# A hybrid transformer block on one core: attention moved in among the qkv slabs, its bias added by VectorE, its forget sums made by a scan

## The chip, the core and the metric

The kernel runs on one NeuronCore of a Trainium2 chip. The metric is the device time of one execution in microseconds (us), lower is better; of several runs the median counts. TensorE is called PE below, VectorE DVE, ScalarE ACT, GpSimd POOL and SyncE SP.

## The reference, cut to what matters

Two layers over 256 positions of width 1024, in float32. The change touches the attention of the first:

```python
h = rmsnorm(x, ln1)
z = h @ w_in     # q, k, v of branches a, b, c, four forget columns fb, gates ga, gb, gc
o_a = moba_attention(qa, ka, va, tbl_a)                     # 4 heads of 64, causal, + bias by distance
o_b = forgetting_attention(qb, kb, vb, fb + b_f)            # 4 heads: logit[t,s] += sum_{s<j<=t} log sigmoid(f_j)
o_c = sliding_window_sink_attention(qc, kc, vc, sinks, tbl_c)  # 8 heads, 2 kv heads, window 128, bias, sink
merged = sigmoid(ga)*(o_a @ w_pa) + sigmoid(gb)*(o_b @ w_pb) + sigmoid(gc)*(o_c @ w_pc)
x = x + merged @ w_o
```

After it come a gated feed-forward part with a short convolution, and the second layer (a recurrence, cross attention, feed-forward).

## The kernel before

The weights are cut into 126 slabs of 128x2048 numbers. SP loads them into four buffers (raw), ACT rounds a slab into w_hi (L442), DVE subtracts to get w_lo (L843), and PE makes three products for each wanted one (L1438 to L1440: hi x hi, hi x lo, lo x hi). w_hi and w_lo have two buffers each, so slab n+2 can be split only when PE has used slab n (slab_used). ACT and DVE work through lists written by hand: a call of splits(m) splits all slabs up to m at that place of the engine's list, and whatever stands behind it waits. The result of a slab is a unit, held in PSUM bank 0 or 1 in turn, and ACT evacuates it.

The order around the change is: slabs 0 to 8 hold q, k and v (L1510 on), the last of them also the keys and values of branch c. Then PE makes the four forget columns with the activations stationary and four columns moving (48 products, L1521 on). DVE and ACT make the logarithm of the sigmoid from them, DVE copies it 128 columns wide (neglog_wide, L930), PE makes running sums with triangular masks (L1533 to L1535). Then follow twelve gate slabs in four batches of three. Sixteen heads go in four groups of four: group 0 is branch a, 1 is b, 2 and 3 are c. scores(g) makes the products of a group one head at a time in banks 2 and 3: queries by keys (L1549, 64 rows deep, fp32), and into the same bank the bias by a product with a mask that turns it around (L1559), or the forget sums (L1553, L1556). DVE copies each head out (L952; L946 and L948 for branch b) and finds the maxima (L957, L958); ACT takes the exponentials (L528); DVE normalises. After the next batch of gate slabs PE transposes the probabilities (prob_transposes, L1568) and multiplies by the values (weighted_values, L1580 and L1581), with ACT's copy of the transposed tile in between (pT, L540). scores(0) stands ahead of the first batch, scores(g+1) right behind the values of group g. The last group's values stand right ahead of stage proj, whose products read the attention's output and whose results DVE multiplies with the gates.

POOL makes the bias: PE and ACT make one row of it per head, POOL writes the rows to memory and reads them back shifted by one per partition (L400 to L406, bias_scratch to bias).

## Time and profile before

| | before |
|---|---|
| median of 3 runs | 1018.44 us (1017.45 to 1018.93) |
| profiled execution, its own time | 1017.91 us |
| its span, first to last instruction | 1015.7 us |
| mean granted TensorE clock | 0.958 |
| PE busy | 921.7 us, 91% |
| DVE, ACT, POOL busy | 569.8 (56%), 446.3 (44%), 17.5 (2%) |

Busy time of PE is that of its matmuls; their ends are modelled, so 91% is not a distance to a peak. A granted clock of 1.00 is 2.4 GHz, one of 0.50 is 1.2 GHz. In a row of the timeline the bracket at the end says how long the engine was idle before and what ended the wait; an fp32 product is two instructions and appears as x2. Times in a window row are of the window only.

### The profile page before, as it was taken

To read this page: it belongs to the slowest core of one execution; us is meant where nothing else is said; L and a number is where in the kernel's file an instruction comes from. 1 tells how busy PE (TensorE), PEld (TensorE's weight loads), DVE (VectorE), ACT (ScalarE), POOL (GpSimd) and SP (SyncE) were. 2 spreads that over 40 slices of the span, in tenths; PEclk is the share of its full clock that TensorE was granted. 3 is DMA by queue.
4 is the path that set the end of the run, shared out by engine and by line. 5 is a ranking of instruction groups with operands and counts; after the bars stand their busy time and mean duration, and the time that the engine had idled before them with its cause. 6 is when DMAs were issued, how large, how long until landed. Compare 5 with 4: busy or idle time off the path is not lost.

```text
span 1015.7 us, 18816 instructions
## 1 busy us (share of the span) xinstructions
PE 921.7 (91%) x8050; PEld 838.3 (83%) x8050; DVE 569.8 (56%) x693; ACT 446.3 (44%) x580; POOL 17.5 (2%) x24
## 2 busy tenths in 40 slices
PE   2998999998979999999898889987898799999996
PEld 1997877787769999988798788876796599999885
DVE  2331434456657787754759987545644545555443
ACT  4342353642455655553537330135544544343433
POOL 1100000000000000000200000000000000000000
PEclk9996899999989999999899999998999989999999
DMA  8651222332544554555453221122440435455541
GB/s 313 230 196 49 84 84 83 125 125 84 171 179 166 181 191 168 194 187 194 149 186 124 86 85 45 47 81 83 152 164 38 167 117 193 165 184 187 185 147 41
DMA packets 20925, 142.93 MB, mean 141 GB/s; under 512 B 2446, under 2 KB 2490, under 8 KB 4608
## 3 DMA queue, kind: packets, MB, share of 16 engines
q1 hardware_dynamic: 18720, 134.23, 38.3%
q0 software_dynamic: 2000, 6.74, 1.9%
q8 instruction: 51, 0.84, 0.3%
q10 hardware_dynamic: 144, 1.05, 0.3%
q14 instruction: 10, 0.08, 0.0%
HBM read 140.94 MB, written 1.07 MB: 140 GB/s over the span
## 4 chain that ended last, share of the span: by engine, by line
PE 75%; DVE 12%; ACT 8%; issue 3%; DMA 1%; SPq 0%; ACTq 0%; DVEq 0%
PE ps L1438 21%; PE ps L1440 20%; PE ps L1439 20%; DVE w_lo L843 4%; ACT w_hi L442 3%; PE ps L1756 2%; PE ps L1549 2%; PE ps L1559 2%; PE ps L1466 1%; PE ps L1706 1%; ACT sc L528 1%; DMA x<-in_x 1%; ACT xn L455 1%; PE ps L1580 1%; DVE xn L1351 1%
## 5 line engine op out<-in xcount | busy, mean ns | idle before, releaser
L843 DVE TENSOR_TENSOR w_lo<-raw,w_hi 128x2048 fp32r<-128x2048 f32 x126 | 289.6, 2299 | 195.2 <-ACT w_hi L442 195.2
L1438 PE MATMUL ps<-hT_hi,w_hi 128*128 128x256 f32 x1240 | 358.4, 289 | 7.0 <-DVE w_lo L843 7.0
L1439 PE MATMUL ps<-hT_lo,w_hi 128*128 128x256 f32 x1240 | 354.9, 286 | 0.0
L1440 PE MATMUL ps<-hT_hi,w_lo 128*128 128x256 f32 x1240 | 354.5, 286 | 0.0
L442 ACT ACTIVATE w_hi<-raw 128x2048 fp32r<-128x2048 f32 x126 | 240.6, 1910 | 153.4 <-PE ps L1440 152.7
L1438 PEld LDWEIGHTS ps<-hT_hi,w_hi 128*128 128x128 f32 x1240 | 242.5, 196 | 11.5 <-issue 10.9
L1439 PEld LDWEIGHTS ps<-hT_lo,w_hi 128*128 128x128 f32 x1240 | 242.4, 195 | 0.2
L1440 PEld LDWEIGHTS ps<-hT_hi,w_lo 128*128 128x128 f32 x1240 | 242.1, 195 | 0.0
L1438 PE MATMUL ps<-w_hi,gT_hi 128*128 128x512 f32 x176 | 69.7, 396 | 0.2 <-DVE w_lo L843 0.2
L1440 PE MATMUL ps<-w_hi,gT_lo 128*128 128x512 f32 x176 | 69.0, 392 | 0.0
L1439 PE MATMUL ps<-w_lo,gT_hi 128*128 128x512 f32 x176 | 68.4, 388 | 0.0
L1438 PE MATMUL ps<-w_hi,hT_hi 128*128 128x512 f32 (+2 forms) x144 | 52.3, 363 | 7.7 <-DVE hT_lo L897 7.7
L1466 PE MATMUL ps<-masks,xn 128*128 128x128 f32 x96 | 19.8, 377 | 42.6 <-DVE xn L880 31.2
L1061 DVE SCALAR_TENSOR_TENSOR ub<-ps,pvec,ub 128x255 f32<-128x255 f32 (+1 forms) x88 | 38.4, 478 | 29.6 <-ACT ub L584 26.7
L1466 PEld LDWEIGHTS ps<-masks,xn 128*128 128x128 f32 x96 | 15.6, 193 | 46.1 <-DVE xn L880 16.5
L1439 PE MATMUL ps<-w_lo,hT_hi 128*128 128x512 f32 (+2 forms) x144 | 52.0, 361 | 0.0
L1440 PE MATMUL ps<-w_hi,hT_lo 128*128 128x512 f32 (+2 forms) x144 | 51.8, 360 | 0.0
L584 ACT ACTIVATE ub<-ps,pvec 128x256 f32<-128x256 f32 x44 | 22.5, 561 | 54.5 <-PE ps L1440 54.5
L1440 PEld LDWEIGHTS ps<-w_hi,gT_lo 128*128 128x128 f32 x176 | 33.0, 188 | 7.7
L1438 PEld LDWEIGHTS ps<-w_hi,gT_hi 128*128 128x128 f32 x176 | 33.1, 188 | 7.4 <-DVE w_lo L843 0.9
L1439 PEld LDWEIGHTS ps<-w_lo,gT_hi 128*128 128x128 f32 x176 | 33.0, 188 | 7.2
L1438 PEld LDWEIGHTS ps<-w_hi,hT_hi 128*128 128x128 f32 x144 | 27.9, 194 | 12.4 <-issue 8.6
(289 smaller groups left out, 1145.0 us busy)
## 6 DMA issues: line engine op xcount, KB each, us to landing
raw<-in_weights SPq DMA_DIRECT2D x126, 1024.0 KB, 4.9
row_gain<-in_rows_vec POOLq DMA_DIRECT2D x4, 512.0 KB, 4.7
bias<-bias_scratch POOLq DMA_DIRECT2D x1, 1536.0 KB, 11.3
masks<-in_masks ACTq DMA_DIRECT2D x1, 1025.5 KB, 7.8
x<-in_x SPq DMA_DIRECT2D x2, 512.0 KB, 8.1
xn<-in_mem POOLq DMA_DIRECT2D x2, 512.0 KB, 4.2
out<-x SPq DMA_DIRECT2D x2, 512.0 KB, 2.6
bias<-bias_scratch POOLq DMA_DIRECT2D x1, 768.0 KB, 6.8
```

Of the source, the lines that this page charges most:

```text
L442: A(w_hi[:, n % SPLIT, :], raw[:, n % RAW, :], ACT.Copy).then_inc(sems["hi_ready"], 1)
L455: A(ub[:, 1, :, :, :].rearrange("p a b n -> p (a b n)") if name == "mem" else xn[:, t, :], src(t), ACT.Square, accum_out=stat[:, 4 * q + t ...
L584: A(ub[:, p % 2, s, c, :], src[:, c * T:(c + 1) * T], ACT.Identity, bias=pvec[:, bass.ds(p + 2 * turn, 1), col + 3], scale=pvec[:, bass.ds ...
L843: V.tensor_tensor(w_lo[:, n % SPLIT, :], raw[:, n % RAW, :], w_hi[:, n % SPLIT, :].bitcast(F32), ALU.subtract).then_inc(sems["lo_ready"], 1)
L1061: ins = V.scalar_tensor_tensor(out=dst, in0=src[:, c * T:(c + 1) * T - lag], scalar=pvec[:, bass.ds(p + 2 * turn, 1), 4 * (2 * s + c) + ta ...
L1438: mm(dst, left[0], right[0], start=first, stop=False)
L1439: mm(dst, left[0], right[1], start=False, stop=False)
L1440: return mm(dst, left[1], right[0], start=False, stop=last)
L1466: last = nc.tensor.transpose(ps[:, transposed_bank(name, k), k % 2 * T + t * P:k % 2 * T + (t + 1) * P], xn[:, t, k * P:(k + 1) * P], ident)
L1549: mm(dst[:, cols], qkT[rows, qtile, qt * P:(qt + 1) * P], qkT[rows, ktile, 0:(qt + 1) * P], start=True, stop=False)
L1559: last = mm(dst[:, cols], m("turn"), bias[:, b, cols], start=False, stop=True)
L1756: last = mm(ps[to, b + q, j * CHUNK:(j + 1) * CHUNK], left[rows, 8 * q + j, :], right(rows, 8 * q + j), start=True, stop=True)
```

## The change

- The order of the columns of w_in is changed, so that the slab with keys and values of branch c is the seventh and the queries of branch c come after it. The forget columns are no longer a unit of their own.
- forget_gates, behind slab 2: the forget columns are stationary (4 wide), the activations move (256 columns), 24 products into bank 6, on four partitions. DVE and ACT make the logarithm there, on 4x256 numbers (tile forget), and DVE makes the running sum with a scan.
- forget_sums, behind slab 4: two products turn the sums into columns and four spread them over 128 partitions in banks 6 and 7. DVE adds both and the causal mask into the score tile of group 1 ahead of its scores.
- scores(g) writes four heads into banks 2 to 5, two heads in turn: one uses rows 0 to 63, the other rows 64 to 127, so that neighbouring instructions use different halves. It makes only the products of queries and keys.
- DVE adds the bias to two heads in one instruction, reading the tile bias backwards along its columns; for group 1 it adds what stands in the score tile already.
- Attention starts behind slab 2: scores(0) there, the values of group 0 behind slab 5, of 1 behind slab 8, of 2 behind the fourth gate slab, of 3 behind the eighth. Four gate slabs follow.
- ACT's and DVE's lists are rewritten to fit. ACT's exponentials of a group are cut into two halves, each of two heads; its splits run one slab further ahead, splits(n0 + i + 2) ahead of the evacuation of unit i.
- The masks cum and turn (384 columns) are no longer loaded; the tile masks keeps the width that the later masks need. The bias rows are stored in the other direction, and POOL's two loads of bias have other widths and the same bytes.

```diff
--- before.py
+++ after.py
-              ("causal", 384), ("cum", 2 * P), ("turn", P))
+              ("causal", 384))
...
-        neglog_wide = sb("neglog_wide", [P, TT, 4, P], F32, attention)
+        forget = sb("forget", [4, 4, T], F32, attention)
...
-            for first, place, width in ((0, P, P), (P, 0, 2 * P)):
-                src = bass.AP(bias_scratch.tensor, place, [[1, P], [BIAS_ROW, 12], [1, width]])
+            for first, width in ((0, 2 * P), (2 * P, P)):
+                src = bass.AP(bias_scratch.tensor, 0, [[1, P], [BIAS_ROW, 12], [1, width]])
                 pool.dma_start(bias[:, :, first:first + width], src).then_inc(sems["bias_in"], 16)
...
+            qkv_parts = ((0, scale), (2, 1.0), ("v", 0), (4, scale), (6, 1.0), ("v", 256), ("kv", 512), (8, scale), (10, scale))
+            def qkv_out(i):
+                dst, s = qkv_parts[i]
...
+            def exps(g, heads):
                 act.wait_ge(sems["negmax_ready"], g + 1)
-                for i in range(4):
+                for i in heads:
                     for qt in range(TT):
                         s, e = (0, P) if qt == 0 else (P, 3 * P)
                         col = qt * 16 + 4 * g + i
                         A(sc[:, g % 2, i, s:e], sc[:, g % 2, i, s:e], ACT.Exp, bias=ast[:, 88 + col:89 + col],
                           accum_out=ast[:, 120 + col:121 + col]).then_inc(sems["probs_ready"], 1)
-                if g >= 2:
+                if g >= 2 and heads[-1] == 3:
...
+            for i in range(3):
+                splits(n0 + i + 1)
+                qkv_out(i)
+            splits(n0 + 4)
+            act.wait_ge(sems["z_ready"], 1)
+            A(forget[:, 1, :], forget[:, 1, :], ACT.Exp).then_inc(sems["e_ready"], 1)
+            act.wait_ge(sems["e_ready"], 1)
+            A(forget[:, 1, :], forget[:, 1, :], ACT.Ln, bias=m("ones_all")[0:4, 0:1]).then_inc(sems["log1p_ready"], 1)
+            for g in range(2):
+                exps(g, (0, 1))
+                for i in range(3 * g + 3, 3 * g + 6):
+                    splits(n0 + i + 2)
+                    qkv_out(i)
+                    if i == 3 * g + 3:
+                        exps(g, (2, 3))
+                outputs(g)
             n0, u0 = FIRST_SLAB["gates"], FIRST_UNIT["gates"]
-            splits(n0 + 1)
-            exps(0)
...
+            for i in range(12):
+                if i in (0, 4):
+                    exps(2 + i // 4, (0, 1))
+                splits(n0 + i + 2)
+                evacuated(u0 + i, A(sig[:, 2 * i:2 * i + 2, :].rearrange("p a n -> p (a n)"), unit(u0 + i),
+                                    ACT.Sigmoid))
+                if i in (1, 5):
+                    exps(2 + i // 4, (2, 3))
+                elif i in (3, 7):
+                    outputs(2 + i // 4)
...
+            n0 = FIRST_SLAB["qkv"]
+            splits(n0 + 4)
+            dve.wait_ge(sems["fb_ready"], 1)
+            do(V.tensor_scalar(forget[:, 0, :], ps[0:4, 6, 0:T], vec[0:4, VEC["b_f"]:VEC["b_f"] + 1], None, ALU.add))
             settle()
-            V.tensor_tensor(ast[:, 32:40], ast[:, 0:8], ast[:, 8:16], ALU.min).then_inc(sems["z_ready"], 1)
-            dve.wait_ge(sems["e_ready"], 1)
...
+            V.scalar_tensor_tensor(out=forget[:, 1, :], in0=forget[:, 0, :], scalar=-1.0, in1=forget[:, 0, :], op0=ALU.mult,
+                                   op1=ALU.min).then_inc(sems["z_ready"], 1)
+            do(V.tensor_scalar(forget[:, 0, :], forget[:, 0, :], 0.0, None, ALU.min))
             def maxima(g):
                 kind, _ = HEAD_GROUPS[g]
                 if g >= 2:
                     dve.wait_ge(sems["pT_ready"], 4 * (g - 1))
-                for i in range(4):
-                    h = 4 * g + i
...
+                for pair in range(2):
+                    dve.wait_ge(sems["scores_ready"], 4 * g + 2 * pair + 2)
+                    dst = sc[:, g % 2, 2 * pair:2 * pair + 2, :]
+                    b = 2 * pair + (0 if kind == "A" else 4 * (g - 1))
+                    added = dst if kind == "B" else bias[:, b:b + 2, ::-1]
+                    V.tensor_tensor(dst, ps[:, 2 + 2 * pair:4 + 2 * pair, 0:384], added, ALU.add)\
+                        .then_inc(sems["scores_freed"], 1)
+                dve.wait_ge(sems["scores_freed"], 2 * g + 2)
...
+            dve.wait_ge(sems["bias_in"], 32)
             maxima(0)
+            dve.wait_ge(sems["log1p_ready"], 1)
+            settle()
+            do(V.tensor_tensor(forget[:, 2, :], forget[:, 1, :], forget[:, 0, :], ALU.subtract))
+            settle()
+            V.tensor_tensor_scan(out=forget[:, 3, :], data0=m("ones_all")[0:4, 0:1].broadcast_to([4, T]), data1=forget[:, 2, :],
+                                 initial=0.0, op0=ALU.mult, op1=ALU.add).then_inc(sems["cum_row_ready"], 1)
+            splits(n0 + 5)
+            normalise(0)
+            dve.wait_ge(sems["cum_ready"], 1)
+            do(V.tensor_scalar(ast[:, 48:56], ps[:, 2, 0:8], -1.0, None, ALU.mult))
+            settle()
+            for i in range(4):
+                for qt, cols in enumerate((slice(0, P), slice(P, 384))):
+                    ins = V.scalar_tensor_tensor(out=sc[:, 1, i, cols], in0=banks(6, 2)[:, i * T:i * T + (qt + 1) * P],
+                                                 scalar=ast[:, 48 + 4 * qt + i:49 + 4 * qt + i], in1=m("causal")[:, cols],
+                                                 op0=ALU.add, op1=ALU.add)
+                    do(ins) if i < 3 or qt == 0 else ins.then_inc(sems["forget_ready"], 1)
+            splits(n0 + 7)
+            outputs(0)
+            dve.wait_ge(sems["forget_ready"], 1)
+            settle()
+            maxima(1)
+            splits(n0 + 8)
+            normalise(1)
             n0 = FIRST_SLAB["gates"]
             splits(n0 + 1)
-            normalise(0)
-            for g in range(4):
-                splits(n0 + 3 * g + 3)
+            outputs(1)
+            for g in (2, 3):
+                maxima(g)
+                splits(n0 + 4 * g - 5)
+                normalise(g)
+                splits(n0 + 4 * g - 3)
                 outputs(g)
-                if g < 3:
-                    maxima(g + 1)
-                splits(n0 + 3 * g + 4)
-                if g < 3:
-                    normalise(g + 1)
+            splits(n0 + 12)
...
+            def qkv_slab(i):
                 if i in (2, 5):
                     bank_free(u0 + i)
                     used(token_narrow(n0 + i, u0 + i, 0, T))
-                elif i == 8:
+                elif i == 6:
                     features(n0 + i, u0 + i, None, tiles=1)
                     used(token_narrow(n0 + i, u0 + i, P, P))
                 else:
                     used(features(n0 + i, u0 + i, FILL["ln1"] if i == 0 else None))
-            pe.wait_ge(sems["fb_split"], 1)
-            bank_free(u0 + 9)
-            for t in range(TT):
+            def forget_gates():
+                pe.wait_ge(sems["fb_split"], 1)
+                pe.wait_ge(sems["bias_row_ready"], 2)
                 for k in range(KD):
                     w = slice(4 * k, 4 * k + 4)
-                    last = three(ps[:, (u0 + 9) % 2, 4 * t:4 * t + 4],
-                                 [part[:, k, t * P:(t + 1) * P] for part in (hT_hi, hT_lo)],
...
+                    last = three(ps[0:4, 6, 0:T], (fbw_hi[:, w], fbw_lo[:, w]), (hT_hi[:, k, :], hT_lo[:, k, :]),
+                                 k == 0, k == KD - 1)
+                last.then_inc(sems["fb_ready"], 1)
+            def forget_sums():
+                pe.wait_ge(sems["cum_row_ready"], 1)
+                pe.wait_ge(sems["scores_freed"], 2)
+                for t in range(TT):
+                    mm(ps[:, 2, 4 * t:4 * t + 4], forget[:, 3, t * P:(t + 1) * P], ident[0:4, 0:4], start=True, stop=True)
+                for i in range(4):
+                    last = mm(banks(6, 2)[:, i * T:(i + 1) * T], ident[0:4, i:i + 1].broadcast_to([4, P]), forget[:, 3, :],
+                              start=True, stop=True)
+                last.then_inc(sems["cum_ready"], 1)
+            def scores(g, after):
                 kind, _ = HEAD_GROUPS[g]
-                for i in range(4):
-                    h = 4 * g + i
...
+                pe.wait_ge(out_freed[after % 2], after // 2 + 1)
+                pe.wait_ge(sems["scores_freed"], 2 * g)
+                if g == 1:
+                    pe.wait_ge(sems["forget_ready"], 1)
+                for pair in range(2):
+                    qtile, ktile = {"A": (pair, 2 + pair), "B": (4 + pair, 6 + pair), "C": (8 + 2 * (g - 2) + pair, 12)}[kind]
                     for qt, cols in enumerate((slice(0, P), slice(P, 384))):
-                        mm(dst[:, cols], qkT[rows, qtile, qt * P:(qt + 1) * P], qkT[rows, ktile, 0:(qt + 1) * P],
-                           start=True, stop=False)
...
+                        for i in range(2):
+                            rows = slice(64 * i, 64 * i + 64)
+                            last = mm(ps[:, 2 + 2 * pair + i, cols], qkT[rows, qtile, qt * P:(qt + 1) * P],
+                                      qkT[rows, ktile, 0:(qt + 1) * P], start=True, stop=True)
+                            if qt:
+                                last.then_inc(sems["scores_ready"], 1)
             def prob_transposes(h):
                 g, i = divmod(h, 4)
@@ -1581,21 +1596,37 @@
                 mm(ps[rows, 6 + o % 2, P:T], v_tok[:, 1, col:col + 64], pT[:, h % 2, T:384], start=False,
                    stop=True).then_inc(sems["pv_ready"], 1)
-            for u in (u0 + 8, u0 + 9):
-                pe.wait_ge(out_freed[u % 2], u // 2 + 1)
...
+            def attend(g):
                 prob_transposes(4 * g)
                 for i in range(4):
                     if i < 3:
                         prob_transposes(4 * g + i + 1)
                     weighted_values(4 * g + i)
-                if g < 3:
-                    scores(g + 1)
+            for i in range(3):
+                qkv_slab(i)
+            forget_gates()
+            scores(0, u0 + 1)
+            qkv_slab(3)
+            qkv_slab(4)
+            forget_sums()
+            qkv_slab(5)
+            pe.wait_ge(sems["forget_ready"], 1)
+            attend(0)
+            scores(1, u0 + 4)
+            for i in range(6, 9):
+                qkv_slab(i)
+            attend(1)
+            scores(2, u0 + 7)
+            n0, u0 = FIRST_SLAB["gates"], FIRST_UNIT["gates"]
+            for i in range(12):
+                used(features(n0 + i, u0 + i, None))
+                if i == 3:
+                    attend(2)
+                    scores(3, u0)
+                elif i == 7:
+                    attend(3)
...
-    dist = 2 * P - 1 - np.arange(BIAS_ROW)
+    dist = np.arange(BIAS_ROW) - (P - 1)
```

## Rows read from the trace of the kernel before

**Rows 1.** The page: busy time by engine; the granted clock in 40 slices.
```profile
PE 921.7 (91%) x8050; PEld 838.3 (83%) x8050; DVE 569.8 (56%) x693; ACT 446.3 (44%) x580; POOL 17.5 (2%) x24
...
PEclk9996899999989999999899999998999989999999
```

**Rows 2.** Windows cut where PE's work changes: us, busy by engine, PEclk, DMA share, GB/s.
```profile
81.33:89.20 7.87, 7.87 (x50) 7.87 (x49) 0.00 (x0) 1.94 (x3) 0.00 (x0) 0.66 0.14 57
89.20:94.11 4.91, 1.49 (x7) 1.39 (x7) 1.68 (x8) 4.04 (x5) 0.00 (x0) 0.50 0.00 2
94.11:108.61 14.50, 14.50 (x34) 8.06 (x33) 1.84 (x4) 0.75 (x1) 0.00 (x0) 0.50 0.00 0
108.61:127.48 18.87, 18.83 (x146) 18.57 (x145) 11.45 (x16) 9.70 (x21) 0.00 (x0) 0.93 0.33 112
127.48:132.88 5.40, 4.61 (x30) 2.95 (x28) 0.42 (x1) 2.51 (x6) 0.00 (x0) 1.00 0.58 197
132.88:141.95 9.07, 9.07 (x42) 6.19 (x41) 2.65 (x7) 3.47 (x3) 0.00 (x0) 1.00 0.00 0
...
166.10:174.17 8.07, 8.07 (x34) 4.76 (x33) 2.10 (x4) 3.46 (x3) 0.00 (x0) 1.00 0.01 2
...
206.69:225.72 19.03, 17.67 (x146) 17.47 (x145) 11.86 (x19) 9.80 (x22) 0.00 (x0) 1.00 0.39 126
225.72:232.13 6.41, 4.68 (x31) 2.95 (x29) 0.85 (x2) 3.41 (x8) 0.00 (x0) 1.00 0.30 124
```

**Rows 3.** Timeline of ACT among the qkv slabs: start, us, line, tiles, idle before.
```profile
61.82 0.60 ACT L508 ACTIVATE v_tok<-ps 128x512 f32<-128x512 f32 x1 [3.36 <-PE ps L1440]
62.31 1.90 ACT L442 ACTIVATE w_hi<-raw 128x2048 fp32r<-128x2048 f32 x1
67.58 0.60 ACT L514 ACTIVATE qkT<-ps 128x512 f32<-128x512 f32 x1 [3.36 <-PE ps L1440]
```

**Rows 4.** Timeline of PE in the scores of group 2, at the full clock.
```profile
166.51 0.49 PE L1559 MATMUL ps<-bias,masks 128*128 128x128 f32 x2
166.93 0.70 PE L1549 MATMUL ps<-qkT 64*128 64x256 f32 x2
167.56 0.70 PE L1559 MATMUL ps<-bias,masks 128*128 128x256 f32 x2
```

**Rows 5.** PE on small tiles: the convolution's window (32x32), a blockwise product (64x64).
```profile
562.00:575.00 13.00, 10.33 (x494) 7.36 (x492) 12.82 (x19) 2.95 (x4) 0.00 (x0) 1.00 0.35 105
...
630.35 1.16 PE L1756 MATMUL ps<-rw 64*64 64x64 f32 x64
```

**Rows 6.** Groups by line and shape: count, busy us, mean ns, idle before.
```profile
L843 DVE TENSOR_TENSOR w_lo<-raw,w_hi 128x2048 fp32r<-128x2048 f32 x11 | 25.2, 2290 | 12.1 <-ACT w_hi L442 12.1
L528 ACT ACTIVATE sc<-sc,ast 128x256 f32<-128x256 f32 x12 | 5.9, 495 | 0.0
L952 DVE COPY sc<-ps 128x384 f32<-128x384 f32 x8 | 4.5, 558 | 11.7 <-PE ps L1559 11.7
L958 DVE TENSOR_REDUCE ast<-sc 128x4 f32<-128x1024 f32 x3 | 3.6, 1208 | 0.0
```

**Rows 7.** Timeline at the start of the values of group 0, ACT and PE.
```profile
128.18 0.87 ACT L540 ACTIVATE pT<-ps 128x384 f32<-128x384 f32 x2
...
128.72 0.65 PE L1580 MATMUL ps<-pT,v_tok 128*64 128x256 f32 x2 [0.41 <-ACT pT L540]
```

**Rows 8.** Timeline of PE: three idle gaps elsewhere, in the bracket.
```profile
244.54 0.55 PE L1438 MATMUL ps<-oT_hi,w_hi 128*128 128x256 f32 x1 [2.37 <-DVE sc L1021]
...
262.39 0.47 PE L1438 MATMUL ps<-w_hi,hT_hi 128*128 128x512 f32 x1 [2.49 <-DVE hT_lo L897]
...
554.31 0.36 PE L1438 MATMUL ps<-hT_hi,w_hi 128*128 128x256 f32 x1 [2.02 <-DVE w_lo L843]
```

**Rows 9.** Windows right behind the first and the last of these gaps.
```profile
244.43:247.84 3.41, 3.29 (x16) 3.33 (x17) 2.36 (x4) 0.00 (x0) 0.00 (x0) 0.51 0.85 286
...
555.04:558.45 3.41, 3.41 (x18) 3.41 (x18) 3.19 (x7) 3.39 (x4) 0.00 (x0) 0.51 0.91 303
```

104 lines of the change are left out of this document (12 added, 92 removed).

## The prediction

> **What bounds the kernel now.** I read the page first. TensorE is busy for 91% of the span [rows 1], so what counts is what stands in TensorE's own order. Then I read TensorE's timeline and cut it where the line changes; that gives the stretches of [rows 2]. The reader is to see three things there. Between the last qkv slab (81.33) and the first product of the proj stage (232.13) lie 150.80 us, and only twelve slabs of gate columns are work of the dense kind: one slab takes 67.58 - 61.82 = 5.76 us at the full clock [rows 3], so 69.1 us. The rest is attention. Second, two stretches stand without slab work: the forget columns (7.87) and the vector work behind them (4.91, TensorE busy for 1.49). Third, the granted clock: 0.66 and then 0.50 from the forget columns on, through all scores of the first group, which take 14.50 us where those of a later group take 8.07 [rows 2].
>
> I add against the profiled execution, 1017.91 us with a span of 1015.7, 2.2 us outside of it. The median of the timed runs is 0.5 us above it.
>
> **Forget columns and their sums.** Removed: 7.87 + 4.91 = 12.78 us [rows 2]. Added, forget_gates: 24 products instead of 48, with 4 stationary columns and 256 moving ones. A product of a slab with 256 moving columns costs 5.76/48 = 0.12 us [rows 3], so 24 x 0.12 = 2.9; I take 2.8. The vector work (sigmoid's logarithm, the scan) moves beside slabs 3 and 4. No row prices a scan fed like this one: between 0 and the 2.29 us of DVE's largest instruction [rows 6]; DVE starts on it only after the split of slab 4 and the maxima of group 0: by the order of its queue the sums are ready some 6 us before TensorE asks for them after slab 4, so both ends are hidden and I cost it at nothing; without this cover it would be the 4.91 us again. Added, forget_sums: four fp32 products of 256 columns and two of 4. The serial price of a 256-column fp32 product is 0.63 [rows 4]; consecutive ones of the same shape should cost less, between 0.3 and 0.6 each: 2.3 in all. The eight additions behind them on DVE (3 us) end some 2 us before slab 5 does. Net: 5.1 - 12.8 = **-7.7**.
>
> **Scores.** Removed: 14.50 + 9.07 + 2 x 8.07 = 39.7 us [rows 2]; groups 2 and 3 are alike. The bias products and the forget products go from TensorE altogether. What is left per group is, for each of two pairs, two heads with 128 and with 256 columns. In [rows 4] a 128-column fp32 product costs 166.93 - 166.51 = 0.42 and one of 256 columns 167.56 - 166.93 = 0.63, so 0.21 per product does not scale with the columns. There a product with 64 rows always alternates with one of 128. One after the other, four heads cost 4 x (0.42 + 0.63) = 4.2 us: the upper end. Now the two heads of a pair take the lower and the upper 64 rows and write two different banks. That such halves run at once is in the trace: 64 instructions of 64x64 took 1.16 us, 18 ns apart [rows 5], and 494 of 32x32 with 256 columns fill 13 us, 26 ns apart, where a 256-column fp32 instruction alone takes about 0.2 (half of 0.42). If only the two heads overlap and the 0.21 stays, a group costs 2 x (0.42 + 0.63) = 2.1; if the 0.21 goes as well, 1.3: the lower end. I take 2.2, nearest to the 64-row rows, so 8.8 for four groups: **-30.9** (from -34.5 to -22.9).
>
> The Trainium skill, page "TensorEngine Tiling (Array Packing)", section "Key Properties", says that changing the tiling mode drains TensorE, while different tiles of one mode work in parallel. The 0.21 us that does not scale agrees with the first, the 64x64 row with the second; by the page alone a group would be at its lower end, and the total 3 to 4 us lower.
>
> **DVE in place of the bias products.** The copy of one head (384 columns out of PSUM) takes 0.56 [rows 6]; the change adds two heads, 768 columns, in one instruction. At most that is 1.12 per pair; some of the 0.56 won't double, so I take 0.95, 1.9 per group. Whether reading the bias from its end costs more no row shows; bounds are 0 and as much again (1.9 per group). Behind it stand the two reductions (1.21 for the longer [rows 6]) and then the exponentials; for the first pair of heads 4 x about 0.45 [rows 6]. From the end of the scores that is 3.5 + 1.9 = 5.4 us until ACT is free to split the next slab, against 5.76 us of the slab that TensorE computes meanwhile. It fits with 0.4 to spare; a doubled read would overrun by 0.5 to 1.5, and the split has 1.5 us of slack (below). Cost: nothing, at most 1 us per group.
>
> **Slabs between.** The gate batches now take 18.87 to 19.03 us instead of 17.3 [rows 2]: four times, 75.7 in all. The cause is ACT, where eight exponentials and two table loads stand ahead of a split. In the new order a slab n+2 is split right at the end of slab n: w_hi 1.9 and w_lo 2.29 us [rows 3, 6], ready 4.25 after that end, needed after 5.76. Slack 1.5. The exponentials go in halves between splits, so I expect 12 x 5.76 = 69.1: **-6.6**. This also needs two more table loads per group, which ACT has time for.
>
> **What attention now waits for.** Before, ACT evacuated the last slab of a batch and copied the first transposed probabilities at once (0.54 ahead of the first value product at 128.72, which had waited 0.41 [rows 7]). Now splits(n0 + i + 2) stands ahead of the evacuation of slab i and of outputs(g) in ACT's queue, and it can't start before slab i is used. It takes about 1.8 us. Queued behind it: the evacuation (0.5), then the copy of pT, and TensorE waits for that copy after its six transposes. So each of the four attention blocks goes from 5.40 [rows 2] to 7.2, with one idle stretch of about 2.2 us in it: **+7.0**.
>
> **Ends.** The attention block no longer stands right ahead of proj: of 6.41 us [rows 2] the 1.0 behind the 5.4 goes, but the evacuation of the last gate slab and its split come to stand ahead of the first multiplication of proj (about +1.1). Loading 384 fewer mask columns (0.2 MB) ahead of the first slab gives between 0 and 0.6; I take 0.4. Together **-0.3**.
>
> Sum without the clock: -7.7 - 30.9 - 6.6 + 7.0 - 0.3 = **-38.5**.
>
> **The clock.** After a gap of 2.37 us the granted clock stood at 0.51 (of 2.4 GHz, so 1.2 GHz), after one of 2.02 as well, but not after one of 2.49, where the page's clock digits stay at 9 around 262 us [rows 1, 8, 9]; the fall came or not with the gap's position. The new idle stretch of 2.2 us lies among these, so each of the four blocks may see a fall; by these three I give each a bit over one half. A fall here is dearer than elsewhere: behind the gap comes fp32 work, and in [rows 2] the half clock lasted through all of the first group's scores and ended only in the slabs behind them. The rest of the block (3.6 us, of which TensorE is busy some 2) grows by 1.9, the scores by 2.2, and until the clock is back some 4.5 us of slab pass at 3.41/16 = 0.213 per product [rows 9] instead of 0.12, a loss of about 2: 6 us per fall. Two falls are the likeliest: **+12**. The old long fall at the forget columns is in the rows removed above; I expect none at the new ones, which follow a slab without idle time and run at a slab's pace per product; the rival below prices the other case.
>
> Total: -38.5 + 12 = -26.5 us. From 1017.91 that is 991.4, from the median 991.9: **992 us**.
>
> **Rivals.**
> No fall: the gaps are short enough. For it: the 2.49 us gap that left the clock alone. Against it: 2.37 and 2.02. Time 1018.4 - 38.5 = 980, with one fall 986. The Trainium skill, "TensorE: Matmul & The Clock Gate", section "Why this matters for your kernels", asks only that gaps between bursts stay below a length that none of the new gaps reaches, which would give this case; here the 2.02 us gap speaks against that rule.
> All four blocks fall, or a fall lasts longer: 1018.4 - 38.5 + 24 = 1004.
> The pairs don't run side by side: scores 4.2 instead of 2.2 per group, 8 us more: 1000 with two falls.
> Slower than before: the clock falls at the new forget columns, as it fell at the old ones without a gap ahead of them (granted 0.66 over 7.87 us [rows 2]), and stays down through the stage. Place: from 44 us to proj. Price: a slab takes 48 x 0.213 = 10.2 instead of 5.76, so 0.44 us are lost per us at half clock; it decides from 38.5/0.44 = 88 us of low clock on. Over the whole stage, 18 slabs, it would be 80 us more: 1060. Against it: over the 18.87 us from 108.61 the granted clock is 0.93 [rows 2], so slabs brought it back after 0.07 x 2 x 18.87 = 2.6 us; the page's clock line shows no long fall behind a slab either [rows 1].
>
> **How the numbers follow.** Forecast (two or three falls, 988 to 999): 0.47. No or one fall: 0.22. All four, or longer: 0.13. No side by side: 0.11. Some wait that I have not seen, which eats most of the gain but leaves over 2 us: 0.03. Slower by the clock: 0.03. No change: 0.01. The low end is no fall with the cheapest scores, 980 - 3 = 977; the high end is four falls and a little more, 1006. Outside I leave 0.1 above and 0.08 below or between. Below 0.2% (2 us) a measurement of this kernel can't tell from no change. Faster 0.96, same 0.01, slower 0.03.
>
> **What would show it.** Scores: first to last row of the score line per group, 2.2 us, no bias products. Attention block: 7.2 with one wait of about 2.2 for the pT copy, and ACT's w_hi ahead of it. Clock: 0.5 in windows right behind some of these gaps, none at the forget columns. Slabs 5.76 apart without waits for w_lo. proj begins near 195 plus the falls. If pairs are over 3 us, the overlap is wrong; if DVE's pair addition is near 2 us, the backward read; if blocks are near 5.4, ACT's order.

## The result and the profile after

| | before | after |
|---|---|---|
| median of 4 runs each, side by side | 1018.68 us (1017.45 to 1022.75) | 986.9 us (984.35 to 987.14) |
| ratio | | 0.9676, 95% interval 0.9644 to 0.9707 |
| span of the profiled execution | 1015.7 us | 985.1 us |
| mean granted clock | 0.958 | 0.963 |
| PE busy | 921.7 us | 893.7 us |

The prediction was 992 us, from 977 to 1006, with 0.96 on faster. The time lies in the range, 5 us below the forecast, 0.5% of the time. The terms of the sum are another matter: one is off by 8.6 us and three by 2 to 4, in both directions.

The page of after, where [rows 1] stood for before:

```profile
PE 893.7 (91%) x7960; PEld 818.4 (83%) x7960; DVE 570.4 (58%) x686; ACT 447.8 (45%) x580; POOL 17.5 (2%) x24
...
PEclk9999999999799999999899999998999799999999
```

The 6 of [rows 1] behind the forget columns has gone. The windows of after, cut where PE's work changes (columns as in [rows 2]):

```profile
43.41:46.25 2.84, 2.84 (x26) 1.93 (x24) 0.20 (x1) 2.62 (x3) 0.00 (x0) 1.00 0.89 283
46.25:47.76 1.51, 1.51 (x17) 1.13 (x16) 1.51 (x1) 1.07 (x1) 0.00 (x0) 1.00 0.45 184
59.45:61.82 2.37, 2.37 (x14) 1.85 (x13) 1.84 (x8) 2.20 (x2) 0.00 (x0) 1.00 0.62 159
61.82:69.16 7.34, 7.34 (x49) 7.34 (x49) 5.06 (x10) 0.20 (x1) 0.00 (x0) 0.77 0.36 115
69.16:77.75 8.59, 6.23 (x30) 3.64 (x28) 2.72 (x2) 4.41 (x7) 0.00 (x0) 0.80 0.60 219
77.75:79.26 1.51, 1.51 (x17) 1.13 (x16) 0.83 (x2) 0.38 (x1) 0.00 (x0) 1.00 0.11 43
...
99.12:107.44 8.32, 6.03 (x30) 3.65 (x29) 2.72 (x2) 4.42 (x7) 0.00 (x0) 0.79 0.62 224
...
108.95:132.09 23.14, 23.14 (x194) 23.14 (x193) 12.70 (x20) 15.11 (x26) 0.00 (x0) 1.00 0.26 91
132.09:139.35 7.26, 4.61 (x30) 2.95 (x29) 2.72 (x2) 4.31 (x7) 0.00 (x0) 1.00 0.64 203
...
163.99:172.30 8.31, 5.94 (x30) 3.49 (x29) 2.72 (x2) 4.48 (x7) 0.00 (x0) 0.79 0.71 233
...
195.43:227.65 32.22, 25.15 (x194) 24.44 (x193) 23.33 (x27) 10.88 (x14) 0.00 (x0) 0.95 0.44 152
```

They are, in order: forget_gates; the scores of group 0; forget_sums; slab 5; the attention block of group 0; the scores of group 1 (those of 2 and 3 take 1.51 us as well, at 1.00); the attention block of group 1; the first four gate slabs; the blocks of groups 2 and 3; the proj stage. Three things to see. The scores take 1.51 us where they took 14.50, 9.07 and 8.07 [rows 2]. The four blocks take 8.59, 8.32, 7.26 and 8.31 us instead of 5.40, and the clock in them is 0.80, 0.79, 1.00 and 0.79. And slab 5 runs at 0.77, with no idle time ahead of it.

What stretches a block is in its first 3 us. PE, then ACT, in the block of group 0:

```profile
69.16 0.81 PE L1583 MATMUL ps<-masks,sc 128*128 128x128 f32 x6
72.24 0.65 PE L1595 MATMUL ps<-pT,v_tok 128*64 128x256 f32 x2 [2.27 <-ACT pT L538]
```
```profile
69.42 1.91 ACT L443 ACTIVATE w_hi<-raw 128x2048 fp32r<-128x2048 f32 x1 [7.40 <-PE ps L1458]
71.23 0.58 ACT L511 ACTIVATE v_tok<-ps 128x512 f32<-128x512 f32 x1
71.71 0.86 ACT L538 ACTIVATE pT<-ps 128x384 f32<-128x384 f32 x2
```

ACT was idle for 7.40 us until slab 5 was used, did the split (1.91), then the evacuation, and only then the copy of pT that PE had been waiting for. All four blocks have this gap, 2.27 us each time.

Where the 30.6 us between the two spans come from, stretch by stretch:

| | predicted | measured |
|---|---|---|
| forget columns and sums | -7.7 | 2.84 + 2.37 - 12.78 = -7.6 |
| scores | -30.9 | 4 x 1.51 - 39.7 = -33.7 |
| gate batches | -6.6 | 69.4 - 75.7 = -6.3 |
| attention blocks, without falls of the clock | +7.0 | 4 x (7.26 - 5.40) = +7.4 |
| falls of the clock in them | +12 | 1.33 + 1.06 + 1.05 = +3.4 |
| qkv slabs | 0 | 58.1 - 56.2 = +1.9 |
| start, wait ahead of proj, proj | -0.3 | -0.9 - 1.0 + 2.0 = 0.1 |
| behind proj | 0 | 757.45 - 753.31 = +4.1 |
| sum | -26.5 | -30.6 |

The last row but one is the surprise: nothing behind proj was changed, yet it takes 4.1 us longer.

### The profile page after: what moved, and what is told of

Read it like the earlier page. It is cut to its first block, busy times and chain, and to the rows that moved or that the text cites. A ratio compares the mean times of both kernels' runs of the same rounds, so it can differ in the third digit from the quotient of the medians.

```text
span 985.1 us, 18634 instructions
## 1 busy us (share of the span) xinstructions
PE 893.7 (91%) x7960; PEld 818.4 (83%) x7960; DVE 570.4 (58%) x686; ACT 447.8 (45%) x580; POOL 17.5 (2%) x24
## 4 chain that ended last, share of the span: by engine, by line
PE 78%; DVE 11%; ACT 6%; issue 3%; DMA 1%; SPq 0%; ACTq 0%; DVEq 0%
PE ps L1456 23%; PE ps L1457 22%; PE ps L1458 22%; DVE w_lo L857 3%; ACT w_hi L443 3%; PE ps L1787 2%; PE ps L1484 1%; PE ps L1737 1%; PE ps L1595 1%; ACT xn L456 1%; DMA x<-in_x 1%; DVE xn L1369 1%; PE ps L1970 1%; DVE x L1372 1%; PE ps L1950 1%
## 5 line engine op out<-in xcount | busy, mean ns | idle before, releaser
L1458 PE MATMUL ps<-w_hi,gT_lo 128*128 128x512 f32 x176 | 69.4, 394 | 0.0
L1079 DVE SCALAR_TENSOR_TENSOR ub<-ps,pvec,ub 128x255 f32<-128x255 f32 (+1 forms) x88 | 38.4, 478 | 31.1 <-ACT ub L598 28.2
```

Of the source, the lines that this page charges most:

```text
L1079: ins = V.scalar_tensor_tensor(out=dst, in0=src[:, c * T:(c + 1) * T - lag], scalar=pvec[:, bass.ds(p + 2 * turn, 1), 4 * (2 * s + c) + ta ...
L1458: return mm(dst, left[1], right[0], start=False, stop=last)
```

## The experiments

Each kernel starts from the changed kernel unless it says otherwise. The kernel before was run beside each group of them: 1017.45, 1018.16, 1017.73 and 1017.7 us.

| kernel | median of its runs, us | runs |
|---|---|---|
| outputs first | 975.93 (975.15 to 977.11) | 4 |
| gap filled | 980.40 (978.02 to 981.71) | 4 |
| bias products back | 998.44 (995.72 to 1003.31) | 4 |
| all scores in one half | 993.08 | 1 |
| one head after the other | 987.54 | 1 |
| constants as wide as before | 987.20 | 1 |
| tile of 1536 bytes put in | 981.50 | 1 |
| outputs first, proj in another order | 975.64 (972.77 to 977.52) | 4 |
| kernel before, profiled again | 1017.70 | 1 |
| outputs first, again | 974.65 (973.13 to 975.97) | 5 |
| the same with proj in another order, again | 971.43 (970.61 to 973.65) | 5 |
| the latter, 32 bytes put in | 968.33 (966.83 to 970.74) | 5 |

**Outputs ahead of the splits.** Is it the order in ACT's queue that stretches the blocks?

```diff
                 for i in range(3 * g + 3, 3 * g + 6):
-                    splits(n0 + i + 2)
+                    if i < 3 * g + 5:
+                        splits(n0 + i + 2)
                     qkv_out(i)
...
                 outputs(g)
+                splits(n0 + 3 * g + 7)
```

The same in the gate loop for i = 3 and 7, and in DVE's list the split that follows goes behind outputs(g) as well.

> The changed kernel with one order turned: for the last slab of a batch ACT evacuates the unit and copies the transposed probabilities first, and splits the slab after next behind that; DVE takes that split behind the maxima of the next group. Theory A (the 2.27 us gap in each attention block is ACT's split ahead of the pT copy): the four gaps of 2.27 shrink to about 0.4, each block to 5.4 us, no fall of the clock in them; stage proj begins 4 x 1.86 + 3.4 = 10.8 us earlier, less up to 0.3 us per group for the later split; about 976.5 in all. Rival B (the gap is the probabilities coming late from DVE, or TensorE's own order): the blocks stay at 7.3 us or more and the time at 987 or above.

Measured: 975.93 us, ratio to before 0.959 (0.9574 to 0.9606). ACT, then three blocks and proj as windows:

```profile
68.75 0.60 ACT L511 ACTIVATE v_tok<-ps 128x512 f32<-128x512 f32 x1 [7.36 <-PE ps L1462]
69.25 0.87 ACT L538 ACTIVATE pT<-ps 128x384 f32<-128x384 f32 x2
...
74.34 1.90 ACT L443 ACTIVATE w_hi<-raw 128x2048 fp32r<-128x2048 f32 x1
```
```profile
68.55:73.95 5.40, 4.61 (x31) 2.95 (x29) 0.42 (x1) 2.51 (x6) 0.00 (x0) 1.00 0.39 161
95.31:100.71 5.40, 4.61 (x31) 2.95 (x29) 0.42 (x1) 2.51 (x6) 0.00 (x0) 1.00 0.49 185
155.92:161.31 5.39, 4.60 (x30) 2.94 (x28) 0.42 (x1) 2.51 (x6) 0.00 (x0) 1.00 0.58 196
102.22:125.62 23.40, 23.36 (x195) 23.19 (x193) 14.88 (x21) 15.89 (x27) 0.00 (x0) 1.00 0.39 135
184.44:216.60 32.16, 25.12 (x194) 24.41 (x193) 23.31 (x27) 10.88 (x14) 0.00 (x0) 0.95 0.45 154
```

The blocks are back at 5.40 us, none with a fall. The split that now comes late costs 23.40 - 23.14 = 0.26 us in a gate batch: it had slack. This is the gain that the change left lying: 11 us for a turn of order.

**The gap filled.** What does a fall of the clock cost, apart from the gap? 18 products of no use go between the first transposes and the first values, so the gap stays as time but not as idle time.

```diff
                         prob_transposes(4 * g + i + 1)
+                    if i == 0:
+                        pe.wait_ge(sems["scores_freed"], 2 * g + 2)
+                        for k in range(18):
+                            mm(ps[:, 2, 0:T], hT_hi[:, k % KD, 0:P], hT_hi[:, k % KD, :], start=True, stop=True)
```

> The changed kernel with 18 useless dense products of 256 columns in each attention block's gap, written to a free bank (they change no result). ACT's order is untouched. Theory A (a fall of the clock is set off by the idle gap and costs about 1.1 us of a block here): the blocks that had a fall (8.6, 8.3 and 8.3 us) come to 7.3 like the one without, some 3.4 us less in all, about 983.5. Rival C (my prediction's price of 6 us per fall): more than 10 us less. Rival D (sparse fp32 work sets off the falls, not the gap): falls stay and the time is 987 or some us more.

Measured: 980.40 us. The block of group 0:

```profile
68.80:76.06 7.26, 6.76 (x51) 5.14 (x51) 2.71 (x2) 4.46 (x8) 0.00 (x0) 1.00 0.50 177
```

7.26 us at the full clock, and all four alike (7.26, 7.26, 7.26, 7.33). Proj begins at 191.33 instead of 195.43 us: 4.1 less, 0.35 of it from an earlier start and 3.4 from the falls. So a fall costs 1.1 us and not 6. The two traces differ by 5.2 us in all, so 1.1 lie behind proj's begin, where falls move from execution to execution; the medians, of two groups of runs, differ by 6.5. The work behind the gap is the same with and without the products of no use, and with them none of the four blocks has a fall: the falls need the idle time, and the fp32 work alone doesn't bring them.

**The bias back on PE.** The mask turn is loaded again, the bias is turned and added by 128-row products between the pairs of products of queries and keys, for groups 0, 2 and 3; DVE only copies. The bias rows are stored as in the kernel before, and scores(0) waits for the bias.

```diff
+                        if kind != "B":
+                            for i in range(2):
+                                b = 2 * pair + i + (0 if kind == "A" else 4 * (g - 1))
+                                last = mm(ps[:, 2 + 2 * pair + i, cols], m("turn"), bias[:, b, cols], start=False, stop=True)
```

> The changed kernel with the bias added by TensorE again (products with the turning mask into the score banks for the branches with a bias; DVE only copies), all else as changed, the heads still side by side. Theory A (0.21 us per product is a price of going from 64-row to 128-row products and back, and is paid once per two products now): per pair two switches each way, so a group takes 1.5 + 4 x (0.21 + 0.43) + about 1, some 5.1 us instead of 1.5: 3 x 3.6 = 11 us more, about 998. Rival E (the price is per product whatever its neighbour): 4 x (0.42 + 0.63) + 1.5 = 5.7 per group, 12.6 us more, near 1000. Rival F (the gain of the scores comes from pairing, and the bias products hide): under 4 us more.

Measured: 998.44 us, 11.5 more than the changed kernel. Group 0:

```profile
45.31:50.55 5.24, 5.24 (x34) 3.63 (x33) 3.96 (x5) 3.31 (x5) 0.00 (x0) 1.00 0.50 158
```

5.24 instead of 1.51 us, 3 x 3.73 = 11.2. That 11.2 and 11.5 agree so well is chance, for the four times spread from 995.72 to 1003.31 us. The two traces differ by 8.8 us; this one lacks the falls in slab 5 and in proj, 3.1 us together. Eight products more cost 0.47 each, a little less than the mean of 0.42 and 0.63 in [rows 4]. Group 2 of the kernel before took 8.07 us for the same sixteen products [rows 2]. So of the 6.6 us saved in such a group 2.8 come from grouping the products by kind and turning the heads together, and 3.7 from the bias leaving PE.

**All scores in one half, and one head after the other.** Do the two halves of the rows run beside each other, and does the order matter? In the first kernel the second head of a pair is computed from the first one's data.

```diff
-                            rows = slice(64 * i, 64 * i + 64)
+                            rows = slice(0, 64)
```

> The changed kernel, but both heads of a pair use rows 0 to 63, so that the second head's scores are computed from the first head's data; number and shape of the products stay. Theory A (the two halves of the rows run at once): a group's scores go from 1.5 us to 2.6 (streaming alone, 4 x (0.21 + 0.43)) or up to 4.2 (if the 0.21 per product comes back); 4 to 11 us more in all. Rival G (what shrank the scores is only that no 128-row product stands between): they stay at 1.5 us.

```diff
-                    for qt, cols in enumerate((slice(0, P), slice(P, 384))):
-                        for i in range(2):
+                    for i in range(2):
+                        for qt, cols in enumerate((slice(0, P), slice(P, 384))):
```

> The changed kernel with one edit: within a pair of heads both query tiles of the first head are multiplied before both of the second, instead of the two heads in turn. Same products, same tiles, only their order. Theory A (two products lie beside each other only where one right after the other uses the other half of the rows): of four products of a pair the middle two overlap, so a group of scores takes between the 1.51 us of the heads in turn and the 2.81 us of the kernel with all in one half, near 2.1 us; four groups, +2.4 us, 989.3 us. Rival (what counts is that both halves are used somewhere near, and TensorE looks further ahead): 1.51 us, 986.9 us. Rival (a second product of the same half holds everything back): 2.8 us, 992 us.

Group 0 in the first and in the second kernel:

```profile
45.90:48.71 2.81, 2.81 (x17) 2.31 (x17) 2.78 (x3) 1.06 (x1) 0.00 (x0) 1.00 0.22 85
```
```profile
46.41:48.02 1.61, 1.61 (x17) 1.23 (x17) 1.61 (x1) 0.99 (x1) 0.00 (x0) 1.00 0.35 137
```

One after the other costs 2.81 us, side by side 1.51: a bit over half. My upper end, 4.2 us, was wrong even for the serial case: without 128-row products between them eight 64-row products need 0.35 each and not 0.52. And my theory for the order fell: with two products of one half in succession the group takes 1.61 and not 2.1 us. For the overlap it is enough that the other half's product is near. The turn of the heads by itself is worth 0.1 us per group.

**What is behind proj: the place of gT.** PE's products, compared start by start, say where over half of the 4.1 us are: in the down stages of both layers, whose products have gT stationary and 512 columns of the weights moving. (The expectation of the last kernel calls gT the moving tile; that was a slip.) A stretch of 143 such products, before and after:

```profile
452.23:484.96 32.73, 32.73 (x144) 26.86 (x143) 17.89 (x15) 12.69 (x14) 0.00 (x0) 1.00 0.51 177
```
```profile
419.35:452.71 33.36, 33.36 (x144) 26.84 (x143) 17.99 (x15) 12.70 (x14) 0.00 (x0) 1.00 0.50 174
```

Full clock in both, no idle time in either: 229 ns per product before, 233 after, and over all 527 such products of a trace 687 ns for three against 700: 2.3 us by these medians, 2.1 when the 527 distances are added up. Other products have not changed: those with hT stationary, whose tiles lie ahead of all that moved, also with 512 moving columns, stand 227 ns apart in both, and those of the cross attention (kmT with q2T, vm with xpT), whose tiles moved with gT, 216 ns. I took the place of the tile in memory for the cause: 384 columns fewer of constants move all that stands behind them. They do, but by 256 bytes and not by the 1536 that the next two expectations name, since the tile masks must hold the later masks too. gT_hi stands at 161600 in the kernel before, at 161312 in the changed one, at 161568 with the wide constants and at 162848 with the tile put in: neither kernel put it back where it had stood.

```diff
-              ("causal", 384))
+              ("causal", 384), ("pad", 384))
```

> The changed kernel with 384 columns of zeros put back into the constants: their transfer is 192 KB longer, as before the change, and every tile that stands behind the constants in the on-chip memory moves back by 1536 bytes a partition. Theory A: the 0.93 us by which the changed kernel ends its first slab earlier come from the shorter transfer, so the first slab ends near 25.1 us instead of 24.22. Theory P (the place of the tile gT in the memory makes the 2.3 us by which the 512-column products of the two wide stages are slower after the change): the three products of a block start again 226, 229 and 232 ns apart instead of 235, 233 and 232, and the time behind the projection is 2.3 us shorter than 757.45 us. Both: 986.9 + 0.9 - 2.3 = 985.5 us. If neither: 986.9 us.

```diff
+        gap = sb("gap", [P, 384])
         vec = sb("vec", [P, VECS])
```

> The changed kernel with an unused tile of 1536 bytes a partition put behind the constants, so that all tiles behind it stand where they stood in the kernel before; nothing more is transferred. Theory P (the place of the tile gT makes the 2.3 us): the start as in the changed kernel (first slab ends at 24.22 us), the products of gT again 226, 229 and 232 ns apart, 757.45 - 2.3 = 755.1 us behind the projection, 984.6 us in all. Rival (the pace comes from something else, such as where the code lies or what runs beside it): 235, 233 and 232 ns as in the changed kernel, 986.9 us. The longer low clock behind the 5.23 us gap at 254.9 us (10.2 us instead of 6.8) should not depend on the place by either theory; if it does come back to 6.8 us, another 1.4 us are gained.

The same stretch in the second of them:

```profile
415.38:448.74 33.36, 33.36 (x145) 26.84 (x143) 17.98 (x15) 12.69 (x14) 0.00 (x0) 1.00 0.50 173
```

700 ns in both: the theory in this form fell. For the start, the first slab product begins at 24.63 us with the wide constants; in the ten traces with the narrow ones it begins between 23.82 and 24.22 (median 24.02), in the two of the kernel before at 24.61 and 25.15. So the shorter transfer is worth 0.6 to 0.8 us. That the kernel with the tile put in came out 5 us faster is no effect of the tile: two of its four blocks had a fall instead of three, and 757.45 us behind proj became 754.6 with other falls there. A single execution of this kernel is good to some 3 us (the two traces of outputs first differ by 3.2 us behind proj's begin); stretches without a fall are good to 0.05.

**Is it the kernel at all?** The only trace with 687 ns was one of the kernel before, so I took a second one.

> The kernel before, unchanged, for a second profile of it. Behind the projection the changed kernel and six relatives of it take 757 us in their traces (754.6 to 761.6), the one trace of the kernel before 753.3 us; 2.3 us of that are 512-column products of gT, 700 ns for three in all seven and 687 ns in the one. Theory E (it belongs to the one execution or its chip): this trace has 700 ns too, and 755.6 us or more behind the projection. Theory K (the changed kernel makes them slower by some way that I have not found): 687 ns and 753.3 us again. The time is 1018 us by both.

```profile
452.04:484.77 32.73, 32.73 (x144) 26.86 (x143) 17.88 (x15) 12.69 (x14) 0.00 (x0) 1.00 0.51 177
```

687 ns again, and 753.2 us behind proj. It is the program. The addresses of the tiles then showed what both paddings had missed: one more line of the diff, which stands in no step of the prediction.

```diff
-        small = sb("small", [P, 12])
+        small = sb("small", [P, 8])
```

The tile loses 16 bytes, and the tiles behind it move by 32, from a multiple of 64 to an odd multiple of 32; so they stand in both padded kernels. The last kernel puts 32 bytes back and changes nothing else in the fastest version (the one of the next heading):

```diff
         small = sb("small", [P, 8])
+        gap = sb("gap", [P, 8])
```

> The kernel with the projection's order turned (971.43 us in its second run), with an unused tile of 32 bytes a partition put behind the tile small. The change made that tile 32 bytes shorter, from 12 columns to 8, so that every tile behind it stands 32 bytes past a multiple of 64 in the changed kernel and in all its relatives so far (gT_hi at 161312 or 162848), and at a multiple of 64 in the kernel before (161600); here gT_hi stands at 161344, a multiple of 64 again, and otherwise not where it stood. Theory B (a 512-column product reads its moving tile slower from an odd multiple of 32 bytes): the three products of gT take 687 ns again instead of 700, as in both traces of the kernel before; 527 products, 2.3 us less, 969 us (968 to 970). Rival (the 13 ns come from something else in the changed program): 700 ns and 971.4 us.

```profile
402.91:435.66 32.75, 32.75 (x145) 26.86 (x144) 17.89 (x15) 12.68 (x14) 0.00 (x0) 1.00 0.51 178
```

687 ns again, over all 519 intervals of the trace. The tile stands at 161344 here and at 161600 in the kernel before; three other places gave 700 ns. What counts in these five is not the place but whether it is a multiple of 64. The time is 968.33 us, ratio to before 0.952 (0.9492 to 0.9547), 3.1 below its parent on another chip; the products of gT account for 2.1 to 2.3 of them. The weight loads themselves take 188 ns in both kernels, so it is the distance of the products that grows and not a record of theirs.

gT is not the only tile that shows it. The products of hTm (256 moving columns, hTm stationary in one half of them and moving in the other) take 355 to 361 ns for three on the mean in the three traces at a multiple of 64, and 367 to 370 in the eleven others. Together with their waits these stretches grow by only 0.3 us. Those of the cross attention moved by the same 32 bytes and kept their 216 ns, and why some products mind and others don't wasn't tried.

**The order in proj.** The proj stage of outputs first has gaps of 1.23, 1.28 and 2.20 us, because ACT splits ahead of the last evacuation and DVE splits ahead of the first multiplications of a slab. In ACT's gate loop i = 11 joins 3 and 7, and in DVE's list:

```diff
-                splits(n0 + (j // 4 + 1 if j < 8 else 3 + (j - 8) // 2) )
+                if j % 4 > 1 or j >= 8:
+                    splits(n0 + (j // 4 + 1 if j < 8 else 3 + (j - 8) // 2))
```

> The kernel with the outputs ahead of the splits (975.93 us), with two more turns of order: ScalarE evacuates the last gate unit ahead of its next split, and VectorE does the first two multiplications of the first and second projection slab ahead of the split of the next one. Theory A: the gaps of 1.23, 1.28 and 2.20 us in the projection go, the split of the third slab then just reaches TensorE in time or comes up to 0.5 us late; 4 us less, 972 us (971.5 to 973). Rival (the later splits only move the gaps to the next slab): 975 to 976 us.

Proj fell to 28.2 us as expected, though not all of its gaps went: 0.86 and 1.71 us are left, so 2.1 of the 4.0 us are gaps. Most of the rest is the fall behind the gap of 2.2 us, which isn't there any more; proj without that fall takes 30.6 us in the trace with the gap filled. And the median stayed: 975.64 against 975.93 us. The profiled execution had a fall right behind proj. Its window there (the same one in a second trace of this kernel stands further below):

```profile
213.51:242.38 28.87, 23.64 (x96) 19.10 (x96) 15.13 (x16) 11.55 (x11) 0.56 (x1) 0.91 0.45 158
```

Whether this is a rule or belongs to the execution needed both kernels on one chip.

> The kernel with the outputs ahead of the splits once more, in more rounds and on the same chip as the next one: 976 us (975.93 us in its first run; before, 1018).

> The kernel with the projection's order turned as well once more, beside the one that it was made from. Its projection takes 28.2 us instead of 32.2 us in the traces; its time was 975.64 us in four runs that lay between 972.77 and 977.52 us, on another chip than the 975.93 us of the kernel that it was made from. Theory A (the 4 us are kept on the average; what took them in the profiled run was where the low clock fell, which moves from run to run): 4 us below the kernel beside it, 972 us. Rival (the gaps that the projection no longer has kept a fall from coming behind it, so the gain is given back there as a rule): equal within 1 us.

```profile
185.25:213.40 28.15, 23.25 (x192) 22.72 (x192) 23.22 (x27) 10.88 (x14) 0.00 (x0) 1.00 0.49 176
213.40:240.63 27.23, 22.01 (x96) 17.92 (x96) 15.14 (x16) 11.56 (x11) 0.56 (x1) 0.99 0.47 165
```

974.65 and 971.43 us, with ranges that hardly touch: 3.2 of the 4 us are there. The comparison of two kernels that ran on different chips, four times each, had hidden it.

## Why the prediction was right or wrong

**Forget columns: right.** 2.84 and 2.37 us stand against 2.8 and 2.3. The scan took 0.68 us, and the running sum was ready at 54.2 us, 5 us ahead of need, where I had said 6.

```profile
53.51 0.68 DVE L992 TENSOR_TENSOR_SCAN forget<-masks,forget 4x256 f32<-4x256 f32 x1
```

**Scores: right in mechanism, the size off by 2.8 us.** I took 2.2 us a group from a price per product that came from rows where 64-row and 128-row products alternate [rows 4], and kept half of the part that doesn't scale. Measured is 1.51, near the lower end of 1.3. The 64-row products among themselves pay little of that part. Going by the Trainium skill, "TensorEngine Tiling (Array Packing)", "Key Properties", the prediction would have stood at its lower end, nearer to what came. Grouping the same sixteen products by kind saved 2.8 us, which agrees with a drain at each change of mode, but up to 1.3 of it can be the overlap of the two heads (2.81 against 1.51), which the kernel before did not have. No run here separates the two or shows the drain itself.

**DVE's addition: right.** Two heads took 0.95 us, as estimated, and reading the bias backwards costs nothing. The form that reads the bias backwards, then the one of group 1 that reads a tile forwards:

```profile
L945 DVE TENSOR_TENSOR sc<-ps,bias 128x768 f32<-128x768 f32 x6 | 5.4, 947 | 0.2
L945 DVE TENSOR_TENSOR sc<-ps,sc 128x768 f32<-128x768 f32 x2 | 1.8, 953 | 0.1
```

**Attention blocks: right.** The step that names ACT's split ahead of the copy of pT gave 7.2 us and a gap of 2.2 (its +7.0 for four blocks should read +7.2); measured are 7.26 and 2.27, and outputs first removes both. It is the best founded step, since it was read from the order of a queue and not from a price.

**The clock: the price wrong by five times, the number of falls about right.** I expected two falls at 6 us; there were three at 1.1. The failed step is "the half clock lasted through all of the first group's scores and ended only in the slabs behind them", which was carried over from [rows 2]: there the work at low clock was sparse (TensorE busy for 1.49 of 4.91 us) and long, here it is a block that is nearly over, and the clock is back ahead of the scores (1.00 in the row of group 1). So of the three parts of the 6 us, block, scores and slab, only the first was paid, with 1.1 instead of 1.9. Carried over was a duration; that it belongs to the work and not to the fall is my reading and wasn't tried. Of my own rows [rows 9] were the nearer ones: 3.41 us at 0.51, then over. In the changed kernel and its five relatives with the 2.27 us gap, 17 of 24 such gaps had a fall behind them; in the five traces with outputs first (three kernels), where 0.41 us are left of the gap, none of 20. The Trainium skill, "TensorE: Matmul & The Clock Gate", "Why this matters for your kernels", asks only that gaps between bursts stay below a length that 2.27 us doesn't reach. That isn't enough here: the clock fell behind 17 such gaps.

**A fall that I had excluded.** Slab 5 runs at 0.77 and takes 7.34 us instead of 5.8; the low clock begins 0.7 us behind forget_sums, without a gap. I had said of the forget products "I expect none at the new ones". It came in the traces of all relatives but two, the ones with the bias products and with all scores in one half, whose first group of scores takes longer. What in forget_sums brings it (its products use 4 rows) wasn't tried; it costs 1.5 us and stays open.

**Ends and slabs.** The gate slabs run at 5.78 us, the term was right. The start gained 0.9 us in the traces (0.6 to 0.8 by the wide constants) against 0.4. Proj grew by 2.0 and not 1.1, and the part that I priced was right: the evacuation that comes late costs 1.23 us. The wait for DVE's first multiplications behind a split was there before (1.37 us, now 1.27). These rows show the two waits after, and the second of them before:

```profile
198.23 0.36 PE L1456 MATMUL ps<-oT_hi,w_hi 128*128 128x256 f32 x1 [1.23 <-ACT sig L566]
201.16 0.36 PE L1456 MATMUL ps<-oT_hi,w_hi 128*128 128x256 f32 x1 [1.27 <-DVE xn L1035]
```
```profile
236.49 0.36 PE L1438 MATMUL ps<-oT_hi,w_hi 128*128 128x256 f32 x1 [1.37 <-DVE xn L1017]
```

The other 0.9 us is the pace of proj's products: three take 340 ns in the trace of before and 357 after. The second trace of the kernel before has 353 and a proj of 30.75 instead of 30.26 us, so part of it belongs to the execution. What sets this pace stays open.

**Behind proj: a term that was missing.** Of 4.1 us, 2.1 to 2.3 come from the 32 bytes, shown by taking them back. 1.4 us come from the clock behind the gap of 5.23 us ahead of the up stage's transposes, a gap that is the same in both kernels. The first 9.1 us behind it, before and after:

```profile
289.66:298.76 9.10, 8.11 (x49) 7.58 (x50) 4.92 (x9) 5.16 (x9) 1.61 (x3) 0.68 0.26 89
```
```profile
254.90:264.00 9.10, 8.11 (x37) 7.57 (x38) 4.92 (x9) 5.16 (x9) 1.61 (x3) 0.50 0.28 91
```

The same gap is followed by 0.68 and by 0.50, so PE gets through 49 or 37 products. It isn't the change: of its relatives some had the one, some the other (one head after the other 0.69; outputs first had 10.2 us of low clock as here in its first trace and 6.8 in its second). The last half us is spread over the second layer, over its small products above all, and wasn't traced.

So the forecast was 4 us too high (by the spans) by errors that partly cancel, and that it came so near is in part luck: the clock 8.6 us too dear and the scores 2.8 too dear on the one side, the missing 4.1 behind proj, the 1.9 in the qkv slabs and 0.4 each in the blocks and at the ends on the other. With the clock at its true price the forecast would have been 983, too low by as much.

## What to carry over

When a step is moved in front of another in one engine's hand-written list, price the list: what the other engine waits for stood third behind a 1.9 us split, and turning the two gave back 11 us, a third of what the whole change gave. Take the price of a fall of the clock from the work that would stand behind the gap, not from the longest fall in the trace. And look at the tiles that a diff makes shorter: a tile that loses 16 bytes moves all behind it by 32, and products in a stage that nobody touched can get slower.

## What the runs showed of the hardware

- A product with 512 moving columns whose stationary tile starts at an odd multiple of 32 bytes takes 233.3 ns instead of 228.9, at the full clock and with no idle time: 687 ns for three in three traces with the tile gT at a multiple of 64, 700 ns in eleven with it at an odd multiple of 32. Products of hTm with 256 moving columns, as the stationary or as the moving tile, changed by some 10 ns for three; those of the cross attention (216 ns) did not.
- A group of scores, eight 64-row fp32 products of 128 and 256 columns, took 1.51 us when the halves alternate by product, 1.61 when they alternate by two, 2.81 all in one half, and 5.24 with as many 128-row products between them.
- A vector addition of 768 fp32 columns from PSUM took 0.95 us with the second operand read forwards or backwards. A scan of 256 columns on 4 partitions took 0.68.
- The same idle gap of 2.27 us was followed by a fall in 17 of 24 cases, and the same gap of 5.23 us by 6.8 or 10.2 us at 0.50, in two executions of one kernel too. What decides it was not found; it makes executions of one kernel differ by some 3 us.
